# A hybrid decoder layer: expert rows dealt over groups 3 to 30, gate products one step forward, and GpSimd in the combine

## What is computed

```python
h = rmsnorm(x, g_norm1) * (1.0 + scale1) + shift1
aq, ak, av, bb, bc, bx, cz, dq, dk, dv, gl = jnp.split(h @ w_in, SPLIT_POINTS, axis=-1)
# ya: differential attention, yb: short convolution, yc: pooling, yd: sliding-window attention
branches = jnp.einsum('bsgc,gcd->bsgd', jnp.stack([ya, yb, yc, yd], axis=2), w_branch)
gates = jax.nn.sigmoid(gl.reshape(Bn, S, N_BRANCH, D_MODEL))
x = x + gate1 * (jnp.sum(gates * branches, axis=2) @ w_o)
h2 = rmsnorm(x, g_norm2) * (1.0 + scale2) + shift2
x = x + gate2 * peer_ffn(h2, w_q, sub_keys, u_experts, v_experts)
return rmsnorm(x, g_final)
```

## Time and profile before

| | |
|---|---|
| median of 3 runs | 1913.63 us (1911.68 to 1915.3) |
| the profiled execution, its own time | 1910.98 us |
| span, first to last instruction | 1909.2 us |
| TensorE busy | 1822.5 us, 95% of the span |
| VectorE busy | 1521.3 us, 80% |
| ScalarE busy / GpSimd busy | 723.8 us, 38% / 754.2 us, 40% |
| moved by DMA | 526.24 MB, mean 276 GB/s |
| mean granted TensorE clock | 0.98 of full |

### The profile page before, as it was taken

The page is one execution under the profiler, slowest core; times in us unless marked ns, Lnnn a source line. Parts: engine busy times, 40 slices in busy tenths (PEclk is TensorE's granted clock), DMA queues, the critical chain, the costliest instruction groups (busy, mean ns, idle before and its releaser), DMA issues. The chain is left out here.

```text
span 1909.2 us, 27338 instructions
## 1 busy us (share of the span) xinstructions
PE 1822.5 (95%) x9796; PEld 1601.6 (84%) x9796; DVE 1521.3 (80%) x2279; ACT 723.8 (38%) x969; POOL 754.2 (40%) x485
## 2 busy tenths in 40 slices
PE   4999979999899899999999999999889999999997
PEld 4888857777787888999999999999768888888886
DVE  7666467776447668989998999999778988898888
ACT  3322234444423321333333456666523333333331
POOL 0000088000032000568888878888233333333330
PEclk7999989999999999999999999999999999999999
DMA  8899377979485071569999979999999999999992
GB/s 312 267 335 322 110 194 225 250 225 265 147 279 151 4 155 22 165 191 274 311 292 307 276 277 346 350 351 345 350 383 389 384 388 390 379 390 390 390 363 79
DMA packets 306616, 526.24 MB, mean 276 GB/s; under 512 B 21691, under 2 KB 211692, under 8 KB 301933
## 3 DMA queue, kind: packets, MB, share of 16 engines
q1 hardware_dynamic: 269676, 391.11, 63.3%
q0 software_dynamic: 36864, 134.23, 20.0%
HBM read 438.75 MB, written 85.99 MB: 275 GB/s over the span
## 5 line engine op out<-in xcount | busy, mean ns | idle before, releaser
L125 PE MATMUL u_s<-h_hi,u_hi 128*128 128x384 f32 x1024 | 348.9, 341 | 7.7 <-POOL u_lo L1966 3.9
L126 PE MATMUL u_s<-h_lo,u_hi 128*128 128x384 f32 x1024 | 344.4, 336 | 0.0
L127 PE MATMUL u_s<-h_hi,u_lo 128*128 128x384 f32 x1024 | 344.1, 336 | 0.0
L125 PE MATMUL v_o<-v_v_hi,v_w_hi 128*128 128x512 f32 x768 | 300.9, 392 | 13.7 <-DVE v_w_lo L2220 5.9
L126 PE MATMUL v_o<-v_v_lo,v_w_hi 128*128 128x512 f32 x768 | 300.2, 391 | 0.0
L127 PE MATMUL v_o<-v_v_hi,v_w_lo 128*128 128x512 f32 x768 | 300.1, 391 | 0.0
L1966 POOL TENSOR_TENSOR u_lo<-u_ut,u_hi 128x1024 fp32r<-128x1024 f32 x79 | 196.9, 2492 | 54.3 <-ACT u_hi L1749 53.4
L125 PEld LDWEIGHTS u_s<-h_hi,u_hi 128*128 128x128 f32 x1024 | 193.4, 189 | 9.4 <-issue 6.9
L126 PEld LDWEIGHTS u_s<-h_lo,u_hi 128*128 128x128 f32 x1024 | 193.5, 189 | 0.0
L127 PEld LDWEIGHTS u_s<-h_hi,u_lo 128*128 128x128 f32 x1024 | 193.1, 189 | 0.0
L1398 POOL DMA_INDIRECT rows_buf<-in_u_experts_dram,few_idx x117 | 160.2, 1369 | 80.7 <-DMA v_gt<-expert_gates 56.8
(11 more groups left out here) (344 smaller groups left out, 4012.9 us busy)
## 6 DMA issues: line engine op xcount, KB each, us to landing
u_raw<-in_u_experts_dram SPq DMA_DIRECT2D x320, 128.0 KB
v_raw<-in_v_experts_dram SPq DMA_DIRECT2D x74, 512.0 KB
v_slot<-in_v_experts_dram SPq DMA_DIRECT2D x54, 512.0 KB
expert_acts<-u_ao SPq DMA_DIRECT2D x64, 384.0 KB
u_raw<-turned_experts SPq DMA_DIRECT2D x24, 1024.0 KB
expert_gates<-u_gs SPq DMA_DIRECT2D x12, 2048.0 KB
v_gt<-expert_gates SPq DMA_DIRECT2D x30, 768.0 KB
w_in_raw<-in_w_in_dram SPq DMA_DIRECT2D x17, 1024.0 KB, 11.8
```

The costliest lines, as they stand in the source:

```text
L125: nc.tensor.matmul(out, w[0], x[0], start=first, stop=False)
L126: nc.tensor.matmul(out, w[0], x[1], start=False, stop=False)
L127: return nc.tensor.matmul(out, w[1], x[0], start=False, stop=last)
```

## The change

It does four things. (1) In the combine, the 148 rows are dealt over groups 3 to 30 (148 over 28 groups, five or six each) and not over 1 to 31; the late rows end with group 18. (2) The first gate product's weight tile is loaded and split at the end of the projection (`gate_raw`, `g_first`); its 24 matmuls stand in two halves before and behind the first two scores, and in unit n comes gate product n + 1 and no longer n. ScalarE's and VectorE's splits move with them; the last gate product, 31, stands before the transposes of head 2. Four tanh buffers take the place of two, SP stores a tanh before it loads the next tile, and the small loads are waited for where they are used (`kd_in` before the fifth unit, `wpool_in` before the pooling products). (3) From group 1 on GpSimd makes the low part of the fourth value tile of each group, behind that group's gathers; VectorE makes the other three. TensorE waits for both, and SP's load into that slot waits for `quarter_ok`. (4) At the end the sums of squares are ScalarE Square instructions, and the last block's halves come before the scaling of block 2.

```diff
+FIRST_GATE_AT = Y_AT + 36 * KB          # phase_project:
+            sp.wait_ge(share_ok, 16 * (NB // 4) - 8)
+            sp.dma_start(gate_raw[:, :, :], w[:, :, NB * BW:NB * BW + P]).then_inc(gate_in, 16)
...
+            act.wait_ge(gate_in, 16)
+            nc.scalar.activation(g_first[0][:, :, :], gate_raw[:, :, :], ACT.Copy).then_inc(gate_hi, 1)
             store(NB - 1, 0)
...
             split_lo(NB - 1, 0)
+            dve.wait_ge(gate_hi, 1)
+            nc.vector.tensor_tensor(g_first[1][:, :, :], gate_raw[:, :, :], g_first[0][:, :, :].bitcast(F32), ALU.subtract)
...
-            split_hi(0)
             exps(0)
+            split_hi(1)
+            tanh(0)
             exps(1)
             for n, (kind, i, h) in enumerate(units):
...
-                split_hi(n + 1)
-                tanh(n)
+                split_hi(n + 2)
+                tanh(n + 1)
...
             scores_in(0)
-            split_lo(0)
             scores_in(1)
             normalise(0)
+            split_lo(1)
             for n in range(NU):
...
-                split_lo(n + 1)
+                split_lo(n + 2)
...
-            pe.wait_ge(sem["small_in"], 80)
+            def first_gate(cs):
+                for c in cs:
+                    ins = three(nc, gate_bank(0), [g[:, c, :] for g in g_first], (keep["h_hi"][:, c, :], keep["h_lo"][:, c, :]), c == 0, c == KD - 1)
+                return ins
...
+            first_gate(range(0, KD // 2))
             scores(0)
             scores(1)
+            first_gate(range(KD // 2, KD)).then_inc(sem["g_mm"], 1)
...
-                gate_product(n)
+                gate_product(n + 1)
...
-LATE_BY = 16
+LATE_BY = 18
+ROWS_FROM, ROWS_TO = 2, NE // P // GT - 2
...
-    return LATE * min(g, LATE_BY) // LATE_BY
+    return LATE * max(0, min(g, LATE_BY) - ROWS_FROM) // (LATE_BY - ROWS_FROM)
...
-    return (NSLOT + LATE) * g // (NE // P // GT - 1) - late_by(g)
+    return (NSLOT + LATE) * max(0, min(g, ROWS_TO) - ROWS_FROM) // (ROWS_TO - ROWS_FROM) - late_by(g)
...
-                        sp.wait_ge(sem["vlo_ok"], t + 1)
+                        if g and t % GT == GT - 1:
+                            sp.wait_ge(sem["quarter_ok"], g)
+                        else:
+                            sp.wait_ge(sem["vlo_ok"], t + 1 if g == 0 else t + 2 - g)
                         values(t + VSLOTS)
...
+                x = GT - 1
+                pool.wait_ge(sem["vhi_ok"], GT * g + GT)
+                nc.gpsimd.tensor_tensor(v_lo[g % 2][:, x, :], v[(GT * g + x) % VSLOTS], v_hi[g % 2][:, x, :].bitcast(F32), ALU.subtract).then_inc(sem["quarter_ok"], 1)
...
+            def squares(n, i, cs, to):
+                act.wait_ge(sem["sum_ok"], n)
+                nc.scalar.activation(sq[:, cs], acc[:, i, cs], ACT.Square, accum_out=to).then_inc(sem["sq_ok"], 1)
...
             def low_values(g):
-                for x in range(GT):
+                for x in range(GT - 1):
...
-                pe.wait_ge(sem["vlo_ok"], GT * g + GT)
+                pe.wait_ge(sem["vlo_ok"], (GT - 1) * g + GT)
+                pe.wait_ge(sem["quarter_ok"], g)
                 pe.wait_ge(sem["wlo_ok"], g + 1)
```

More of the change, by code:

```diff
@@ L625, in phase_mix @@
         lo = [kg.sb(f"lo{j}", [P, KD, P], F32R) for j in range(2)]
-        th = [kg.sb(f"th{j}", [P, S]) for j in range(2)]
+        th = [kg.sb(f"th{j}", [P, S]) for j in range(TANHS)]
         assert kg.at <= Y_AT + 40 * KB
@@ L661, in _ @@
         def _(sp):
[L662 to L665, removed]
             def load(n):
@@ L672, in rows_in @@
                     sp.dma_start(u_raw[t % 2][32 * q:32 * q + 32, :, :], u[turned_tile(IN_PROJECT + t), q]).then_inc(sem[f"u_in{t % 2}"], 16)
-            load(0)
             load(1)
+            load(2)
+            for g in range(2):
+                for half in range(2):
+                    sp.dma_start(kd[half * HD:(half + 1) * HD, g, :], xt[g * HD:(g + 1) * HD, M_DK, :]).then_inc(sem["kd_in"], 16)
             rows_in(0)
             rows_in(1)
+            sp.dma_start(wpool[:, :, :], a["w_pool"][0].rearrange("g c e -> c g e")).then_inc(sem["wpool_in"], 16)
             sp.wait_ge(sem["g_lo"], 1)
-            load(2)
+            load(3)
             for n in range(NG):
@@ L692, in _ @@
                         load_branch(sp, a, b_first[j], 1, j).then_inc(first_in[j], 16)
[L693 to L697, removed]
+            for j in range(TANHS):
+                sp.wait_ge(th_out[j], 16 * (NG // TANHS))
+            sp.wait_ge(sem["kd_in"], 64)
+            sp.wait_ge(sem["wpool_in"], 16)
         @block.gpsimd
@@ L913, in _ @@
             turn_rows(NU + 1)
-            split_lo(NU + 2)
+            split_lo(NU + 3)
             rstd_dve_in(nc, sem["ssq_ok"], ssq[:, :], fin[:, :], root[:, :], FLT_MAX * SQ_DOWN)
-            for n in range(NU + 3, NU + 6):
-                turn_rows(n - 1)
+            for n in range(NU + 4, NU + 7):
+                turn_rows(n - 2)
                 split_lo(n)
@@ L2085, in phase_combine @@
         p_a = k.ps("a", [P, D])
[L2086 to L2087 removed]
+        names = ("w_in1 gt_in0 gt_in1 wl0_ok w0_ok hi0_ok gf_in vhi_ok vlo_ok quarter_ok w_ok whi_ok wlo_ok mm "
+                 "sum_ok sq_ok ssq_ok root_ok y_ok out_ok dg_ok wg_ok add_ok").split()
         sem = {n: k.sem(n) for n in names}
@@ L2369, in program @@
         turned = nc.dram_tensor("turned_experts", [AHEAD // 2, P, 2 * D], F32, kind="Internal").ap()
-        spent = phase_project(nc, a, keep, xt, y_hi, w_raw, w_in, w_hi_ok, w_lo_ok, turned, spent, acc_w, mm)
+        kg = Kit(nc, top, "first_gate", FIRST_GATE_AT + 4 * KB)
+        g_first = [kg.sb(n, [P, KD, P], F32R) for n in ("hi", "lo")]
+        spent = phase_project(nc, a, keep, xt, y_hi, w_raw, w_in, w_hi_ok, w_lo_ok, turned, spent, acc_w, mm, g_first)
         early.close()
```

117 lines of the change are left out of this document (64 added, 53 removed).

## The result

| | before | changed |
|---|---|---|
| median (range, executions) | 1912.94 us (1911.68 to 1915.3, 4) | 1897.26 us (1896.44 to 1897.82, 4) |
| ratio, 95% interval | | 0.9916 (0.9899 to 0.9933) |
| span of the profiled execution | 1909.2 us | 1894.9 us |
| mixing, first GpSimd pass to the next phase's first ScalarE pass | 241.45 to 502.39: 260.94 | 242.72 to 498.61: 255.89 |
| combine, start of its first matmul to start of its last | 1363.19 to 1897.62: 534.43 | 1360.12 to 1886.57: 526.45 |

The change is faster by 15.7 us; 1896 was forecast, in a range of 1889 to 1905. By place the 14.3 us of the span are 5.05 of mixing (9.1 forecast), 7.98 of the combine (5.7) and 3.1 of the end (2.9), less 1.3 ahead of mixing and 0.7 between mixing and the combine, which the change does not touch.

What follows compares the result with a forecast made beforehand. TensorE, busy 95%, was taken as the bound, so only closing its gaps or shortening the end counts: mixing 9.1 + rows 5.7 + end 2.9 = 17.7 us, median forecast 1896 us, own range 1891 to 1902, wider range 1889 to 1905.

Steps and rivals of the forecast that it cites:

- Transposes at 251.7 ... 3.2 us: Start of mixing: the first transposes come at 251.7 and not 254.9, 3.2 us earlier.
- the clock should hold: 1.4 us: Start of mixing: TensorE idles some 1.5 us, not 10, so its clock stays full and the product takes 1.4 us less.
- I take 4.4, for GpSimd's pooling passes run beside the small VectorE passes there: Start of mixing: the gains make 4.6 us together, taken as 4.4 because of GpSimd's passes.
- From there every unit has one product ... so the lead is carried: Mixing's units: TensorE is full with one product per unit, so the 4.4 us lead lasts to the phase's end.
- the bounds: Mixing: GpSimd holding up a VectorE pass can lose another 2.3 us or win as much: 6.8 to 11.4.
- Rival (c): Mixing does not carry its lead: loads and DMA set its end, 9.1 shrinks to 2, 1903 us; 7%.
- I am wrong if ... the gate phase starts less than 5 us earlier: Sign against the forecast: the phase after mixing, expected some 9 us earlier, starts less than 5 us earlier.
- 5.8 or 1.6; the middle, 3.8: Combine: TensorE's shortfall once the DMA is the pace, 5.8 us at 386 GB/s or 1.6 at 390; 3.8 taken.
- Rival (a): Combine: the DMA has room, so the whole 9.5 us stay and the time is 1892 us; 12%.
- (b): Combine: the DMA gives all back at 380 GB/s, rows gain 0, 1902 us, or 1906 with low mixing and end; 14%.
- GpSimd's part: Combine: GpSimd's low part delays low weights by 1.1 to 1.3 us; no gain while the DMA is the pace.
- rival (d): Combine: GpSimd is the new, slower pace, up to 1.6 us of wait per group, costing 45, 1923 us; 4%.

Runs made afterwards that it cites:

- mix_alone: The kernel before with only the mixing part of the change: 1906.55 us, ratio 0.9964, mixing phase 255.05 us.
- after_split: The changed kernel with GpSimd's long product in mixing (128x2048) cut into four over 128x512: 1897.07 us, ratio 0.9925.
- after_late: The changed kernel with GpSimd's pooling passes held back until the first scores are normalised: 1895.24 us, ratio 0.9911.
- after_tanh_first: The changed kernel with ScalarE's last tanh of mixing ahead of the output of head 2: 1895.81 us, ratio 0.9898.
- rows_alone: The kernel before with the rows dealt over groups 3 to 30 and nothing else: 1906.23 us, ratio 0.9965.
- end_alone: The kernel before with only the new end (ScalarE square sums, block 2 scaled behind the last half): 1910.48 us, ratio 0.9989.
- after_extra_load: The changed kernel with 256 KB more loaded in each of combine groups 1 to 28: 1916.47 us, ratio 1.0011.
- rows_and_gpsimd: The kernel before with rows over groups 3 to 30 and GpSimd's low part of every fourth tile: 1905.83 us, ratio 0.9961.
- after_no_gpsimd: The changed kernel with all four low parts made by VectorE again: 1896.84 us, ratio 0.9919.

## Why the prediction was right, and where it was not

**Start of mixing, wrong in size.** "Transposes at 251.7 ... 3.2 us" measured 2.1, "the clock should hold: 1.4 us" held in two traces (*mix_alone*, *after_split*) and not in that of the change, and the lead taken as 4.4 was 2.05 (3.4 in those two). Seven traces have this start of mixing; in all TensorE idles 2.6 us ahead of the transposes, and the granted clock in product 1 is 1.00 in two of them and 0.75 to 0.80 in five. What decides between them no run shows. The step that failed is "I take 4.4, for GpSimd's pooling passes run beside the small VectorE passes there": 0.2 us for what *after_late* shows to be 2.5. The 3.2 without GpSimd was too low in its turn: in *after_late* the transposes come 4.6 us earlier than before. In the kernel before the two passes of the first unit ran unhindered beside another GpSimd pass:

```profile
254.17 0.29 DVE L869 TENSOR_SCALAR mix_sm<-mix_sm,mix_r 128x128 f32<-128x128 f32 x1
...
253.52 1.49 POOL L729 TENSOR_SCALAR mix_pad<-mix_pad 128x508 f32<-128x508 f32 x1
```

The second took 0.35 us. Moved earlier, they met two TENSOR_TENSORs of GpSimd (L737) and were held.

**"From there every unit has one product ... so the lead is carried", wrong.** The lead of 2.05 us was gone by the sixth unit, behind the long product (-0.1, and -0.3 from the ninth on), and 1.1 came back at the end of the phase: of 2.05 + 5.44 us a net 1.3 were lost. The mechanism and its size (up to 2.3 us more) were in the bounds, not in the sum. A larger lead fared no better: 3.4 us in *mix_alone* were 0.1 behind the long product, 5.85 in *after_late* were 1.2. What mixing kept is the product taken out of its row of units, 5.4 us. Rival (c), a lead that is not carried, had the fact but not the cause: VectorE's list, lengthened by GpSimd, not loads, as *after_late* shows.

**End of mixing.** 0.7 us were taken for the later store and 1.17 found; *after_tanh_first* gives 1.0 of them back. All three together: 2.05 + 5.44 - 1.27 - 1.17 = 5.05 us, under the low bound of 6.8. By a sign that the prediction itself set ("I am wrong if ... the gate phase starts less than 5 us earlier") this part failed: that phase starts at 498.61 us and not at 502.39, 3.8 earlier.

**Combine, right in mechanism, one term over-sized.** Nine rows taken from the first groups removed both waits (*rows_alone*). From the combine's first matmul on, the low weights of group 4 are ready 11.2 us earlier, where 12.2 less 1.2 were forecast. The lead at group 4 was taken as 3.2 us and is 3.42; the DMA as pace was to use it up from group 13 to 20 on, and it was used up at group 20. The shortfall then was "5.8 or 1.6; the middle, 3.8": it is 1.6, the sum of what groups 4 to 30 took over 16.32 us each, nearly all of it from group 20 on, since the DMA runs at 390 to 391 GB/s and not between 386 and 390. The 386 of the earlier trace rows was that one trace. *mix_alone* and *end_alone* have the same rows in the same groups as before, and moved in 1450 to 1650 us:

```profile
DMA packets 37341, 77.98 MB, mean 390 GB/s; under 512 B 2184, under 2 KB 21492, under 8 KB 37338
...
DMA packets 37202, 78.04 MB, mean 390 GB/s; under 512 B 2171, under 2 KB 21388, under 8 KB 37199
```

Why before moved 1% less there no run shows. Rival (a) is out, *after_extra_load* shows no room above 391; so is (b).

The Trainium skill (DMA: Bandwidth & Descriptors, § Where 436 GB/s comes from) has the ports' ceiling at 435 GB/s; this mix of tile loads and gathered rows stopped at 390 to 391 with more wanted, and the measurement decides.

**GpSimd's part, right that it is worth nothing**, by *rows_alone* against *rows_and_gpsimd* and by *after_no_gpsimd*. The cost was placed right in every second group only: low weights 0.93 us longer for 1.1 to 1.3. In the others the lock fell on the weighing, which the forecast did not have. TensorE never waited for GpSimd, so rival (d) is out; its time was also added up wrong, 45 us above 1896 are 1941 and not 1923.

The Trainium skill (SBUF — State Buffer, § SBUF: two separate sides) has the exclusive lock; the pair that ends at 281.44 and 281.45 agrees, and so do VectorE's passes once GpSimd is out of the way. The 0.29 and 0.35 us beside L729 above do not agree with a lock held for the whole of every such GpSimd instruction, though spans on GpSimd are rough.

**End, right**: 5.9 us forecast and 5.93 found.

The errors of mixing (4.0 too much) and of the combine (2.3 too little) cancelled in part, so that the median came out 1.3 us from 1896 is partly luck.

## What to carry to other kernels

Ahead of moving a short chain of dependent VectorE passes, look at what GpSimd does at the new moment: beside 5 us of its work TensorE waited 2.3 us whether it was in one piece or four, and a later start of GpSimd's list was what helped, if only in part. Do not count on a lead to last through a row of units in which another engine is nearly full; work taken out of the row stays gained. Take a DMA rate from more than one trace, and test the limit by adding a load that hardly anybody waits for. Spread traffic so that each group's bytes at the measured rate stay under TensorE's time: 5.3 rows used a lead up, 5.1 kept it.

## What the hardware showed that was not expected

Cutting a GpSimd pass into four gave nothing back. A VectorE pass with one input is held as well: L880, a TENSOR_SCALAR over 128x128, took 1.15 us beside GpSimd's additions (L737) and 0.28 without, and 0.29 beside GpSimd's TENSOR_SCALAR (L729, before), while VectorE's transposes (L402, 1.23 to 1.24 us) and reductions kept their time beside GpSimd's work.
The Trainium skill (SBUF — State Buffer, § SBUF: two separate sides) counts to those that take the lock, beside operations with two SBUF inputs, VectorE's operations in a two-port mode. No row here shows the mode of L880; that it is held fits, that it is not held beside L729 does not.
And 4% more bytes in a group turned a kernel 0.84% faster than before into one 0.11% slower.
